# Routing expert weights in a two-block network kernel: half of the tokens by indirect DMA, half by one-hot matmuls

## The reference

```
q = h_normed @ w_query                     # 8 heads, two halves of a key each
scores = q_half @ subkeys_half             # 128 scores for i, 128 for j, for each head
(i, j), s = top 16 of the sums of the top 16 of each half, for each head
w = softmax(s)                             # 16 weights for each head
out = sum over the 8 * 16 chosen experts of  w * gelu(h_normed . U[i, j]) * V[i, j]
```

## Time and profile before

| | |
|---|---|
| median of 3 runs | 1916.57 us (1916.21 to 1916.73) |
| profiled execution, its own time | 1917.12 us |
| profiled execution, span from first to last instruction | 1915.3 us |
| PE busy | 1633.3 us, 85% |
| PE weight load busy | 1405.8 us, 73% |
| DVE busy | 1244.2 us, 65% |
| ACT busy | 878.6 us, 46% |
| POOL busy | 537.7 us, 28% |
| mean granted clock of the PE | 0.936 |
| DMA | 326.66 MB, mean 171 GB/s |

### The profile page before, as it was taken

How to read it: one execution, slowest core, us unless ns; L and a number is a source line. 1 busy time by engine, 2 the same in 40 slices (tenths; PEclk the granted TensorE clock), 3 DMA queues, 4 the chain that set the end, 5 groups by cost and what they waited for, 6 DMA issues and landing times.

```text
span 1915.3 us, 28883 instructions
## 1 busy us (share of the span) xinstructions
PE 1633.3 (85%) x9800; PEld 1405.8 (73%) x9800; DVE 1244.2 (65%) x2274; ACT 878.6 (46%) x1431; POOL 537.7 (28%) x319
## 2 busy tenths in 40 slices
PE   9999799999999500006999999999999999999998
PEld 8998699999888400005666676669888887878887
DVE  7887588889666200004666666667787787668777
ACT  5665445555444100003444444446655554555554
POOL 1100007888888888881000000000100000000000
PEclk9999999999999855557999999999999999999999
DMA  6777656767666322226666666764456565436663
GB/s 215 273 267 256 236 181 177 177 175 182 193 186 187 44 0 0 0 0 192 206 208 214 209 210 212 232 202 165 134 190 194 186 196 165 135 121 205 190 188 120
DMA packets 144505, 326.66 MB, mean 171 GB/s; under 512 B 51120, under 2 KB 69296, under 8 KB 144048
## 3 DMA queue, kind: packets, MB, share of 16 engines
q1 hardware_dynamic: 101232, 303.33, 49.4%
q0 software_dynamic: 41472, 16.93, 7.5%
q10 hardware_dynamic: 1728, 5.45, 0.9%
HBM read 306.11 MB, written 19.01 MB: 170 GB/s over the span
## 4 chain that ended last, share of the span: by engine, by line
PE 28%; POOL 26%; issue 19%; DVE 12%; ACT 9%; DMA 4%; ACTq 1%; DVEq 1%; SPq 0%; POOLq 0%
POOL routed L752 26%; PE ps L1192 8%; ACT high L805 7%; PE ps L1194 4%; DVE arena L2024 3%; DVE low L1630 3%; PE ps L1222 2%; PE ps L1224 2%; PE ps L1226 2%; DMA raw<-in_w_mix 2%; PE ps L1172 2%; PE ps L1174 2%; PE ps L1173 2%; PE ps L1205 1%; DMA raw<-in_w_query 1%
## 5 line engine op out<-in xcount | busy, mean ns | idle before, releaser
L805 ACT ACTIVATE high<-raw 128x1024 fp32r<-128x1024 f32 (+1 forms) x517 | 536.8, 1044 | 543.5 <-DMA raw<-in_v_tab 234.3
L1630 DVE TENSOR_TENSOR low<-raw,high 128x1024 fp32r<-128x1024 f32 (+1 forms) x516 | 621.7, 1210 | 175.7 <-ACT high L805 171.5
L752 POOL DMA_INDIRECT routed<-h_tok x256 | 497.1, 1942 | 145.0 <-issue 77.8
L1192 PE MATMUL ps<-x_parts,high 128*128 128x512 f32 x1184 | 419.6, 398 | 0.0
L1222 PE MATMUL ps<-high,yl 128*128 128x512 f32 x640 | 212.3, 413 | 242.6 <-DVE yl L1640 239.0
L1172 PE MATMUL ps<-x_parts,low 128*128 128x256 f32 x1328 | 379.1, 285 | 8.0 <-DVE low L1630 7.1
L1173 PE MATMUL ps<-x_parts,high 128*128 128x256 f32 x1328 | 376.4, 283 | 0.0
L1174 PE MATMUL ps<-x_parts,high 128*128 128x256 f32 x1328 | 376.3, 283 | 0.0
L1222 PEld LDWEIGHTS ps<-high,yl 128*128 128x128 f32 x640 | 109.1, 189 | 307.3 <-DVE yl L1640 266.4
L1194 PE MATMUL ps<-x_parts,low 128*128 128x256 f32 x1184 | 332.3, 281 | 0.0
L726 POOL TENSOR_TENSOR stats<-stats 128x1 f32<-128x1 f32 x14 | 8.0, 568 | 963.2 <-DVE stats L1671 963.2
(11 more groups left out here) (337 smaller groups left out, 1615.3 us busy)
## 6 DMA issues: line engine op xcount, KB each, us to landing
raw<-in_u_tab SPq DMA_DIRECT2D x128, 512.0 KB
raw<-in_v_tab SPq DMA_DIRECT2D x128, 512.0 KB
raw<-in_ffn_in SPq DMA_DIRECT2D x88, 512.0 KB
raw<-in_w_mix SPq DMA_DIRECT2D x56, 512.0 KB
raw<-in_ffn_out SPq DMA_DIRECT2D x44, 512.0 KB
routed<-arena POOLq DMA_DIRECT2D x32, 512.0 KB, 6.6
h_tok<-routed SPq DMA_DIRECT2D x128, 128.0 KB, 2.3
raw<-in_w_query SPq DMA_DIRECT2D x16, 512.0 KB
```

The costliest lines, as they stand in the source:

```text
L752: pool.indirect_dma_start(entries, bass.IndirectOffsetOnAxis(ap=slot_index[:, n:n + 1], axis=0), slot_weight[:, n:n + 1], None, compute_op ...
L805: a.activation(w_high(p, 0, n), cols(raw, p, 0, n), ACT.Copy).then_inc(slot_high[p.slot], 1)
L1192: pe.matmul(bank(b).rearrange("p (h t) -> p h t", h=2), cols(high, p, k * PARTS, PARTS), both[:, :, k, :], start=(k == 0), stop=False)
L1630: v.tensor_tensor(w_low(p, 0, n), cols(raw, p, 0, n), w_high(p, 0, n).bitcast(F32), ALU.subtract).then_inc(slot_low[p.slot], 1)
```

## The change

It has these parts.

1. The indirect DMAs scatter only tokens 0 to 127 (128 DMAs instead of 256), into a table of 128 x 128 x 128 floats (8 MB). With one tile left, the 16 DMAs of a head wait for the landing of the 16 just issued for the head before.
2. Clearing takes 16 DMAs of 512 KB: one after `xc_ready` and one after `merged_ready` in each mixer round.
3. The keys are loaded behind the mixer pieces and ahead of the w_out pieces, without the wait for `merged_ready`; the selection's scratch moves to higher columns of arena, and so the U blocks are computed in their natural order.
4. Tokens 128 to 255 are routed by matmuls. PE transposes the chosen weights, i and j of these tokens (3 transposes). For each token, a one-hot matrix of i (slot by i) and a one-hot matrix of j times the weight (slot by j) are built with compares against an iota; their product over the 128 slots is the token's 128 x 128 table. Four tokens are a group with one PSUM bank; there are 32 groups (`GROUPS`). DVE builds the four i matrices in one compare and three of the j matrices, ACT the fourth (Abs, then Relu).
5. The last 64 U blocks run as 32 pairs, each with `project_in` in one PSUM bank, without the sum of halves. From the third pair on, groups are placed behind the pairs, one or two each. Of a finished group, DVE multiplies the columns of the blocks already computed in arena (`group_of(g, 0, j)`), and ACT copies the table's values into the columns of the blocks yet to come; when such a pair comes, gelu goes to PSUM and DVE multiplies it into arena (`pair_of`).
6. In V, `weigh` covers 128 tokens (a load of 64 KB instead of 128 KB) and stands before `ahead(piece_v(j))`. `weigh(0)`, `weigh(1)` and `weigh(2)` move to the last pair of U and behind it.

The core of the diff, without the declarations:

```
-ZERO_PARTS = 32
+ZERO_PARTS = 16
+PAIRS, LEAD = (NKEYS - EARLY) // 2, 3
+GROUPS = PARTS // 4
+        def groups_until(p):
+            return min(GROUPS, max(0, (p - LEAD + 1) * GROUPS // (PAIRS - LEAD)))
+        def group_of(g, j, j_end):
+            t = PARTS + first_of(g)
+            return arena[:, :].rearrange("p (j t) -> p j t", t=SEQ)[:, j:j_end, t:t + 4].rearrange("p j t -> p t j")
...
@@ SP
+            sp.dma_start(keysT, keys).then_inc(keys_loaded, 16)
             for k in range(KC):
                 load(Piece("mix_out", k), w_out[k])
-            sp.wait_ge(merged_ready, KC)
-            sp.dma_start(keysT, keys).then_inc(keys_loaded, 16)
...
                 if j == 0:
-                    for b in range(TB):
-                        sp.wait_ge(scattered[b], 16 * SLOTS)
+                    sp.wait_ge(sel_turned, 1)
+                    sp.wait_ge(scattered, 16 * SLOTS)
+                if j == 2:
+                    sp.wait_ge(group_done, GROUPS)
@@ POOL
             for c in range(KC):
+                pool.wait_ge(xc_ready, c + 1)
+                pool.dma_start(cleared[2 * c], zeros).then_inc(zeroed, 16)
                 pool.wait_ge(merged_ready, c + 1)
-                for n in range(c * ZERO_PARTS // KC, (c + 1) * ZERO_PARTS // KC):
-                    pool.dma_start(cleared[n], zeros).then_inc(zeroed, 16)
+                pool.dma_start(cleared[2 * c + 1], zeros).then_inc(zeroed, 16)
...
-                for b in range(TB):
-                    if h >= 1:
-                        pool.wait_ge(scattered[b], 16 * 16 * h)
-                    for n in range(b * SLOTS + 16 * h, b * SLOTS + 16 * h + 16):
-                        pool.indirect_dma_start(...)
+                if h >= 1:
+                    pool.wait_ge(scattered, 16 * 16 * h)
+                for n in range(16 * h, 16 * h + 16):
+                    pool.indirect_dma_start(...)
@@ ACT
+            def distance(g):
+                t = first_of(g) + 3
+                a.activation(one_hot_w[g % 2][3], iota, ACT.Abs, scale=-1.0, bias=of_j[:, t:t + 1]).then_inc(distance_ready, 1)
+            def act_hot(g):
+                t = first_of(g) + 3
+                a.wait_ge(distance_ready, g + 1)
+                a.activation(one_hot_w[g % 2][3], one_hot_w[g % 2][3], ACT.Relu,
+                             scale=minus_weight[:, t // 4:t // 4 + 1], bias=weight[:, t:t + 1]).then_inc(act_hots_ready, 1)
+            for p in range(PAIRS):
+                first, second = piece_u(EARLY + 2 * p), piece_u(EARLY + 2 * p + 1)
+                ahead(first)
+                t = SEQ - 4 * groups_until(p)
+                a.wait_ge(slot_done[second.slot], second.done)
+                ins = a.activation(pair_of(p, 0, t), pair_bank(p, 0, t), ACT.Gelu_apprx_tanh)
+                if t < SEQ:
+                    ins = a.activation(pair_bank(p, t, SEQ), pair_bank(p, t, SEQ), ACT.Gelu_apprx_tanh)
+                ins.then_inc(gelu_ready, 1)
+                if p == PAIRS - 1:
+                    coef_high_part(0)
+                ahead(second)
...
+                for g in range(groups_until(p), groups_until(p + 1)):
+                    a.wait_ge(group_done, g + 1)
+                    if g + 2 < GROUPS:
+                        distance(g + 2)
+                    j = EARLY + 2 * (p + 1)
+                    a.activation(group_of(g, j, NKEYS), scattered_group(g)[:, :, j:], ACT.Copy).then_inc(group_copied, 1)
+                    if g + 2 < GROUPS:
+                        act_hot(g + 2)
+            coef_high_part(1)
@@ PE
+            for p in range(PAIRS):
+                if p == LEAD - 1:
+                    ...
+                    for n, chosen in enumerate((slot_weight, slot_i, slot_j)):
+                        ins = pe.transpose(bank(0, n * PARTS, PARTS), chosen[:, 1], ident)
+                pe.wait_ge(gelu_ready, EARLY + p - 3)
...
+                for half in range(2):
+                    project_in(piece_u(EARLY + 2 * p + half), bank(4 + p % 4, half * SEQ, SEQ))
+                for g in range(groups_until(p), groups_until(p + 1)):
+                    pe.wait_ge(one_hots_ready, g + 1)
+                    pe.wait_ge(act_hots_ready, g + 1)
...
+                    for u in range(4):
+                        ins = pe.matmul(bank(g % 4, u * PARTS, PARTS), one_hot[g % 2][:, u * PARTS:(u + 1) * PARTS],
+                                        one_hot_w[g % 2][u], start=True, stop=True)
+                    ins.then_inc(group_done, 1)
@@ DVE
+            def one_hots(g):
+                t = first_of(g)
+                v.tensor_tensor(one_hot[g % 2].rearrange("p (t i) -> p t i", t=4),
+                                of_i[:, t:t + 4].unsqueeze(2).to_broadcast([PARTS, 4, PARTS]), iota4, ALU.is_equal)
+                for u in range(3):
+                    ins = v.tensor_scalar(one_hot_w[g % 2][u], iota, of_j[:, t + u:t + u + 1],
+                                          weight[:, t + u:t + u + 1], ALU.is_equal, ALU.mult)
+                ins.then_inc(one_hots_ready, 1)
+            for p in range(PAIRS):
+                if p == LEAD - 1:
+                    v.wait_ge(sel_ready, 2)
+                    one_hots(0)
+                    one_hots(1)
+                ahead(piece_u(EARLY + 2 * p))
+                v.wait_ge(gelu_ready, EARLY + p + 1)
+                if p == PAIRS - 1:
+                    weigh(0)
+                t = SEQ - 4 * groups_until(p)
+                if t < SEQ:
+                    v.tensor_tensor(pair_of(p, t, SEQ), pair_of(p, t, SEQ), pair_bank(p, t, SEQ), ALU.mult).then_inc(pair_weighed, 1)
+                if p == PAIRS - 1:
+                    weigh(1)
+                    coef_low_part(0)
+                ahead(piece_u(EARLY + 2 * p + 1))
+                for g in range(groups_until(p), groups_until(p + 1)):
+                    v.wait_ge(group_done, g + 1)
+                    if g + 2 < GROUPS:
+                        one_hots(g + 2)
+                    j = EARLY + 2 * (p + 1)
+                    v.wait_ge(group_copied, g + 1)
+                    v.tensor_tensor(group_of(g, 0, j), group_of(g, 0, j), scattered_group(g)[:, :, 0:j], ALU.mult).then_inc(group_weighed, 1)
+            weigh(2)
+            coef_low_part(1)
 
             def outer_step(j, it):
                 if j + 2 < NKEYS:
                     coef_low_part(j + 2, it)
+                if j + 3 < NKEYS:
+                    weigh(j + 3, it)
                 if j < NKEYS - 2:
                     ahead(piece_v(j, it))
-                if j + 3 < NKEYS:
-                    weigh(j + 3, it)
```

More of the change, by code:

```diff
@@ L390, in build @@
         small = [part(mx + 4200 + 8 * n, KC) for n in range(5)]
[L391 to L405, removed]
+        keysT = part(21504, 16 * PARTS)
+        tk = 23552
+        qs = part(tk, 4 * SEQ)
+        sc = [part(tk + 1024 + 1024 * n, 1024) for n in range(2)]
+        rest = part(tk + 3072, 1024)
+        cand, cand2 = part(tk + 4096, 1024), part(tk + 5120, 1024)
+        eqs = part(tk + 6144, 1024)
+        top1, idxf = part(tk + 7168, 128), part(tk + 7296, 128)
+        idxu = part(tk + 7424, 128).bitcast(U32)
+        posu = part(tk + 7552, 64).bitcast(U32)
+        digit = part(tk + 7616, 64).bitcast(U32)
+        digitf = part(tk + 7680, 64)
+        best = part(tk + 7744, 64)
+        first_place = part(tk + 7808, 32)
+        expsum = part(tk + 7840, 32)
         v_tok = part(0, TB * D)
@@ L621, in _ @@
                 for k in range(it * OF_ROUND, (it + 1) * OF_ROUND):
[L622 to L627, removed]
+                    load(piece_u(k), u_tab[k])
+            for k in range(EARLY, NKEYS):
+                load(piece_u(k), u_tab[k])
             def outer_step(j, it):
@@ L2003, in _ @@
                     chain.wait()
-                    chain.step(v.tensor_reduce(places4[:, n], eqs4, AX.X, ALU.add))
+                    chain.step(v.tensor_reduce((slot_i, slot_j)[n][:, :, heads], by_place, AX.X, ALU.add))
                 chain.wait()
-                for b in range(TB):
-                    first, second = (chosen[:, 64 * n + 32 * b:64 * n + 32 * b + 32] for n in range(2))
-                    ins = v.tensor_scalar(first, first, 2.0 * PARTS, token[:, b:b + 1], ALU.mult, ALU.add)
-                chain.step(ins)
+                chain.step(v.tensor_scalar(first_place, slot_i[:, 0, heads], float(PARTS), token, ALU.mult, ALU.add))
                 v.wait_ge(exp_ready, it + 1)
@@ L2013, in _ @@
                 link(v.reciprocal(sums, sums))
+                v.scalar_tensor_tensor(out=slot_index[:, heads], in0=slot_j[:, 0, heads], scalar=float(PARTS * PARTS), in1=first_place,
+                                       op0=ALU.mult, op1=ALU.add)
                 for b in range(TB):
-                    first, second = (chosen[:, 64 * n + 32 * b:64 * n + 32 * b + 32] for n in range(2))
```

(11 more changed lines are left out.)

111 lines of the change are left out of this document (57 added, 54 removed).

## The result

The changed kernel takes 1647.31 us in the median of 4 runs (1645.72 to 1648.41), the kernel before 1916.39 in the same rounds; the ratio is 0.8596, 95% interval 0.8581 to 0.8611. The forecast was 1653.5 in a range of 1640 to 1692. The profiled execution took 1647.26 us with a span of 1645.1, which is 270.2 less than before.

A forecast was written before the change was run, and what follows sets the result against it. Routing was taken to bound the kernel from 648 to 879 us. Terms -14 + 3.8 + 28.2 + 0.7 - 231.3 + 2.7 - 53.2 = -263.1 gave 1653.5 us; own range 1643 to 1664, 8-in-10 range 1640 to 1692.

The forecast's parts named there:

- The hole: Between U and V, PE stands still 231.3 us waiting for routing; the change removes it, leaving 2.7 us.
- the three entries a pair: Second half of U: POOL gets in three indirect DMAs per 6.73 us pair, 2.24 us each; 2.73 was taken instead.
- The 604: Scatter's end near 604 us if multiplies with PSUM input leave POOL alone; the forecast itself took 638.
- The late date: Latest time for the scatter's end, from PE wanting V block 1 at about 672: 665 us, leaving 27 us.
- Routing is still late: Rival, chance 0.22: the scatter ends 13 or 36 us late at the end of U, total 1666 or 1690 us.
- U's second half: PE pays +3.8 us for pieces in project_in, +28.2 for group matmuls, +0.7 for transposes; ACT and DVE keep up.
- the warning that the prediction sets beside this step: Trainium skill on DVE's arena accesses: every element on another 16-byte line loses time, no figure given; forecast added no cost.
- The seam: From U to V, a small chain from the last gelu through weigh and coef steps costs PE 2.7 us.
- the ring: In V, ACT and DVE wait for each other, setting 3.1 us a piece; weigh before low opens it, -53.2 us.
- another bound: Rival, chance 0.07: V's pace stays near 3.12 us a piece for another reason, +51 us, total 1704.
- Mixer and projection: Start to first scatter: 6 us gained in the mixer from fewer zeros, 8 in the projection, together -14.
- three clears fewer beside them: Projection: query loads run with three fewer clears alongside; given no size of its own within the 8 us gain.

The follow-up runs named there:

- The tripled multiply: Changed kernel with the strided DVE multiply of each group done three times: 1671.11 us, ratio 0.8714.
- the late scatter: Changed kernel with 6 more indirect DMAs a head, 48 in all, into a table nothing reads: 1693.57 us, ratio 0.8839.
- leaving three out of four: Changed kernel with only one of the four one-hot matmuls of each group: 1626.51 us, ratio 0.8482.
- the two edits of order: In V, weigh(j + 3) moved ahead of the next piece's low in the kernel before (1867.21 us), and moved back behind it in the changed kernel (1679.76 us).
- the kernel before with the order alone: Kernel before with one edit, weigh(j + 3) ahead of the next piece's low in V: 1867.21 us, ratio 0.9741.
- The doubled clears: Changed kernel with 16 MB cleared again, four DMAs of 512 KB behind merged_ready in each mixer round: 1662.37 us, ratio 0.8669.
- the late keys: Changed kernel with the keys loaded behind w_out and behind the wait for the mixer's end, as before: 1653.95 us, ratio 0.8629.

## Why the prediction was right, point by point

**The hole.** Right in mechanism and size (-229.3 for -228.6). Routing with 128 DMAs landed near 598, where I had 638. Of these 40 us, 6.5 are the earlier start. For the rest, of my two paces, 2.73 from before and the three entries a pair, the second was the true one: without the three waits for landing in the second half (8.0 us) it was (148 - 8) / 64 = 2.19 us, where three in a pair make 2.24. The 604 worked out from it was close, if a little low by its own terms (454 + 3.93 x 38.8 = 607). The tripled multiply showed why. The landings cost 3.0 us each, my lower value.

**The late date** was the step that failed without showing in the time: 665 was worked out from PE's want of V block 1, and the queue of ACT wants it some 16 us earlier. The slack was then 649 - 598 = 51 us where I had 27, since the scatter was 40 us sooner. "Routing is still late" had 0.22; the kernel stands 51 us from it, and the late scatter shows that its price is real.

**U's second half.** Right: +32.4 for +32.7. The product's 0.22 us is confirmed by leaving three out of four (0.217). DVE was less well sized. By its groups of instructions a pair with groups has 2.45 + 0.29 + 1.10 x (0.68 + 0.94 + 1.09) = 5.7 us of work for my 5.2: the strided multiply is 0.52 dearer, three compares together 0.10 of busy time, and the pair's multiply cheaper (0.29 for 0.45). DVE's busy time as a whole, in which the overlap of neighbours counts once, is 147.46 / 193 x 6.73 = 5.1 us a pair, so the slack I had was there, partly by luck. The nearest row to a strided operand was a packed one, and the long form was a factor of 2.0 off: the warning that the prediction sets beside this step was right in direction, and the price stayed inside the slack.

**The seam.** 1.98 us for 2.7. That its slow clock costs another 1.7 us or so I had not counted; it stands in V's time, and in the sum the two nearly cancel.

**V.** Right: the ring was what the two edits of order show it to be, -52.3 for -53.2. The rival "another bound" is refuted by the kernel before with the order alone, which moves 244 GB/s at 2.72 us.

**Mixer and projection.** Here is nearly the whole error: -20.5 for -14, which is 6.5 of the 7.1 us by which the sum is off. Up to the last gate load it was -8.6 (171.73 to 163.09), where I took 6; behind it -11.8, where I took 8 and bounded at 9. With the border at PE's first w_out matmul, which is at 180.58 now and was here in the kernel before, the two parts are -9.3 and -11.2:

```profile
189.89 0.71 PE L1222 MATMUL ps<-high,merged_l 128*128 128x512 f32 x2
```

What failed is the step "three clears fewer beside them", which I left without a price of its own. The doubled clears put 5.3 us on it (4.7 with the second border), the late keys 8.6; the two overlap. With my own bounds and a seam of 1 us the low end of the forecast's own range is 1646.8 and not 1643, so 1647.3 lies at its very edge. That clears are spread over the round, which the change does, has no part in it.

## What to carry to other kernels

When an engine counts as busy, but a step takes longer than it does where the inputs have piled up (here 3.12 us against 2.72), look for a ring of helpers that wait for each other: follow one step through the queues of the helpers, and see which instruction stands ahead of the one that the ring needs. Work with slack (here `low`) belongs behind work that feeds the next step (here `weigh`), and a deadline is to be read from the queue of each engine that touches the late data, not only from the engine that is the bound. A short wait at a border of stages can cost twice its length, if the clock falls with it.

## What the runs showed of the hardware that I had not expected

- After 1.98 us of standing still PE's granted clock was 0.51 from 663.0 to 666.3 us, a pair of matmuls took 1.05 us instead of 0.62, and full pace was back at 666.3. Without the wait the clock stayed at 1.00.
- A DVE multiply of 504 elements with a step of 256 floats took 1.34 us when it read and wrote SBUF so and 1.06 when it only read so; packed, 512 took 0.69.
- A compare and multiply on 128 columns with two per-partition scalars took 0.37 us, where a multiply with one took 0.28.
- An indirect DMA of 128 single floats took POOL 1.54 us at the least, whether 8 MB or 16 MB of table stand behind it. Landing took 2.4 to 3.7 us behind POOL's end with the DMA engines some 70% busy, 3.0 in the idle hole of the kernel before, and 1.5 at the end of the late scatter (693.6 to 695.1).
- A float32 matmul of 128 columns cost PE 0.22 us; the same in the rounded format 0.11 to 0.12, about as much as one of 256 columns in that format (2.88 / 24 = 0.12).
